# Gate and up projections with the high and low activations side by side in one 512-column matmul, and v in two contraction halves

## The chip, the core and the metric

The kernel runs on one core of a Trainium2 chip. The metric is the device time of one execution in microseconds (us). Engines are named as in the profile: PE is TensorE (matmuls; PEld is its weight load), DVE is VectorE, ACT is ScalarE, POOL is GpSimd, SP is SyncE, which here only issues transfers.

## What is computed

A decoder trunk of two layers on x of 256 tokens by 1024 channels, in float32. Each layer has four token mixers fed by one input projection, sigmoid gates, an output projection, and then a SwiGLU feed-forward part:

```python
for l in range(DEPTH):                       # DEPTH = 2, D = 1024, S = 256, FF_DIM = 2816
    xn = rms_norm(x, norm_mix_g[l])
    proj = xn @ w_in[l]
    xa, q, k, v, zc, xd = jnp.split(proj, splits, axis=-1)      # v: 512 columns
    ...
    merged = (gates[:, :, 0] * (ya @ w_proj_a[l]) + gates[:, :, 1] * (yb @ w_proj_b[l])
              + gates[:, :, 2] * (yc @ w_proj_c[l]) + gates[:, :, 3] * (yd @ w_proj_d[l]))
    x = x + merged @ w_o[l]
    hn = rms_norm(x, norm_ffn_g[l])
    gu = hn @ w_ffn_in[l]                                       # 1024 x 5632
    x = x + (jax.nn.silu(gu[..., :FF_DIM]) * gu[..., FF_DIM:]) @ w_ffn_out[l]
return rms_norm(x, final_norm_g)
```

## The kernel before

Every large product is made of three products in the fp32r type. A weight and an activation are each split into a high part (rounded to fp32r) and a low part (the rest), and the kernel adds hi x hi, hi x lo and lo x hi in PSUM. The weight's high part is a copy by ACT (`split` in the ACT block), its low part a subtraction by DVE (L1077); each is one instruction on 128 x 2048 elements. The activations' parts, `act_hi` and `act_lo`, are made once a layer half (L555, L1100), the feed-forward product's, `ff_hi` and `ff_lo`, once a step (L543 through `ffn_hi`, L1358).

The weights pass through the core in units of 1 MB, 69 a layer, in a ring of three slots (`RING`). For unit u, SP loads `raw` once DVE has split the slot's last tenant (`lo_ready`), ACT makes `w_hi` once PE has used the slot (`w_used`), DVE makes `w_lo`, and PE multiplies. Each engine's order is written out by hand, and each works strictly in that order. A unit whose output is transposed has two halves f of 128 output channels, 8 contraction tiles k of 128 and three matmuls of 256 columns (the tokens) for each, 48 in all (`unit`, L753 to L755 in `mm3`). v and sgu_v come out in token order, with the activations as the stationary operand and 256 weight columns moving (`unit_natural`, L798 to L800); v is units 7 and 8, of 256 columns each.

A layer's order on PE: 11 units of the input projection (banks u % 4), 12 gate units, the branch projections, the last 4 gate units, 4 units of the output projection, then the feed-forward part of 11 steps j. A step is a gate unit, an up unit and a down unit (`ffn_in` twice, `ffn_out`), the down unit one step behind: gate j+1, up j+1, down j. Gate and up use banks 0 and 1 in even steps, 2 and 3 in odd ones; the down units add into banks 4 to 7 through the whole part. Between unit 19 and the last gate units stand the small matmuls of attention, pooling and convolution (`misc`). The pooling and half of the convolution's 31 taps are POOL's (L455, L461, L464, L497 to L510), beginning again with `xa`, which DVE scales out of unit 10's bank; PE transposes the result at unit 20 (L920).

The step-0 gate unit of a layer is multiplied as its activations arrive, in four parts of two contraction tiles (`unit_early`, `unit_pair`). After it comes `norm_stat` (L826, the sum of squares over the channels, from DVE's L1110), after the up unit `norm_rms` (L836, the inverse norm broadcast to all partitions, from DVE's `norm_scale`, L1116 to L1120); ACT copies it to `rms_b`. The norm's factor is applied on the way out of PSUM:

```python
def scaled(out, b, l):
    return V.tensor_tensor(out, low(b), rms_b[:, :, :].to_broadcast([P, 2, S]), ALU.mult)
```

A step's evacuation: DVE scales the gate bank into `ff_g` (L1125), ACT applies Silu in place (L691), DVE scales the up bank into `ff_u`, multiplies (L1353), ACT makes `ff_hi`, DVE `ff_lo`. Between these DVE and ACT split a unit's weights each (`ffn_unit` in both blocks).

## Time and profile before

| | |
|---|---|
| median of 3 runs | 867.55 us (865.9 to 867.69) |
| the profiled execution | 866.84 us, of which 865.2 us span |
| PE busy | 836.9 us, 6971 matmuls |
| DVE, ACT, POOL busy | 610.8, 412.3, 225.5 us |
| granted TensorE clock, mean | 0.991 |
| moved by DMA | 152.3 MB, mean 176 GB/s |

The span is the time from the first to the last recorded instruction. Busy time of PE counts matmuls that overlap once; the duration of one (about 0.28 us) is longer than the distance between the starts of two, since they are pipelined, so the distance of starts is the thing to read. The granted clock is 1.0 at 2.4 GHz and 0.5 at 1.2 GHz. In the views of time, a bracket behind an instruction gives its engine's idle time ahead of it and who ended it; an instruction without one followed at once.

### The profile page before, as it was taken

To read this page: it belongs to the slowest core of one execution; us is meant where nothing else is said; L and a number is where in the kernel's file an instruction comes from. 1 tells how busy PE (TensorE), PEld (TensorE's weight loads), DVE (VectorE), ACT (ScalarE), POOL (GpSimd) and SP (SyncE) were. 2 spreads that over 40 slices of the span, in tenths; PEclk is the share of its full clock that TensorE was granted. 3 is DMA by queue.
4 is the path that set the end of the run, shared out by engine and by line. 5 is a ranking of instruction groups with operands and counts; after the bars stand their busy time and mean duration, and the time that the engine had idled before them with its cause. 6 is when DMAs were issued, how large, how long until landed. Compare 5 with 4: busy or idle time off the path is not lost.

```text
span 865.2 us, 17632 instructions
## 1 busy us (share of the span) xinstructions
PE 836.9 (97%) x6971; PEld 828.1 (96%) x6971; DVE 610.8 (71%) x716; ACT 412.3 (48%) x496; POOL 225.5 (26%) x224
## 2 busy tenths in 40 slices
PE   3999999999999999999989999999999999999995
PEld 3999999999999999999989999999999999999995
DVE  5889988786785556455487999887677665556554
ACT  4554666534554344434365466654346443344332
POOL 7806899156000000000000559952300000000000
PEclk9999999999999999999989999999999999999998
DMA  7694654467465555545447654545645456554621
GB/s 249 197 291 118 185 171 163 147 185 216 145 219 167 177 194 171 207 157 194 148 157 237 189 150 147 147 147 195 195 146 196 160 191 202 176 194 162 208 92 50
DMA packets 124035, 152.30 MB, mean 176 GB/s; under 512 B 3728, under 2 KB 113634, under 8 KB 123968
## 3 DMA queue, kind: packets, MB, share of 16 engines
q1 hardware_dynamic: 121200, 148.38, 53.6%
q0 software_dynamic: 1328, 1.81, 1.0%
q10 hardware_dynamic: 1440, 1.20, 0.5%
q8 instruction: 44, 0.72, 0.3%
q14 instruction: 23, 0.19, 0.1%
HBM read 148.23 MB, written 1.05 MB: 173 GB/s over the span
## 4 chain that ended last, share of the span: by engine, by line
issue 38%; PE 36%; POOL 21%; DMA 2%; POOLq 1%; ACT 1%; DVE 0%; DVEq 0%; ACTq 0%
PE bank L753 12%; PE bank L754 12%; PE bank L755 12%; POOL conv_a L464 7%; POOL gates L461 6%; DMA pool_w<-in_pool_w 2%; POOL gates L503 1%; DMA ifreq<-inv_freq 1%; POOL angles L436 1%; POOL conv_a L455 1%; POOL gates L499 1%; POOL conv_a L510 1%; POOL gates L435 1%; POOL gates L432 0%; POOL rows L476 0%
## 5 line engine op out<-in xcount | busy, mean ns | idle before, releaser
L1077 DVE TENSOR_TENSOR w_lo<-raw,w_hi 128x2048 fp32r<-128x2048 f32 x138 | 328.9, 2385 | 141.9 <-ACT w_hi L543 141.5
L753 PE MATMUL bank<-act_hi,w_hi 128*128 128x256 f32 x1472 | 421.4, 286 | 7.0 <-DVE act_lo L1100 6.6
L754 PE MATMUL bank<-act_lo,w_hi 128*128 128x256 f32 x1472 | 418.2, 284 | 0.0
L755 PE MATMUL bank<-act_hi,w_lo 128*128 128x256 f32 x1472 | 418.0, 284 | 0.0
L543 ACT ACTIVATE w_hi<-raw 128x2048 fp32r<-128x2048 f32 x138 | 263.6, 1910 | 206.9 <-PE bank L755 175.0
L753 PEld LDWEIGHTS bank<-act_hi,w_hi 128*128 128x128 f32 x1472 | 284.1, 193 | 9.3 <-DVE act_lo L1100 7.3
L754 PEld LDWEIGHTS bank<-act_lo,w_hi 128*128 128x128 f32 x1472 | 284.2, 193 | 0.1
L755 PEld LDWEIGHTS bank<-act_hi,w_lo 128*128 128x128 f32 x1472 | 284.1, 193 | 0.0
L754 PE MATMUL bank<-ff_lo,w_hi 128*128 128x256 f32 x352 | 99.1, 282 | 0.0
L753 PE MATMUL bank<-ff_hi,w_hi 128*128 128x256 f32 x352 | 99.1, 281 | 0.0
L755 PE MATMUL bank<-ff_hi,w_lo 128*128 128x256 f32 x352 | 99.0, 281 | 0.0
L753 PE MATMUL bank<-y_hi,w_hi 128*128 128x256 f32 x288 | 81.7, 284 | 0.0
L755 PE MATMUL bank<-y_hi,w_lo 128*128 128x256 f32 x288 | 81.5, 283 | 0.0
L754 PE MATMUL bank<-y_lo,w_hi 128*128 128x256 f32 x288 | 81.5, 283 | 0.0
L455 POOL TENSOR_TENSOR conv_a<-conv_h,par 128x256 f32<-128x256 f32 x2 | 5.4, 2715 | 285.0 <-DVE conv_h L1174 285.0
L464 POOL TENSOR_TENSOR conv_a<-conv_a,gates 128x256 f32<-128x256 f32 x60 | 65.9, 1099 | 4.7
L753 PEld LDWEIGHTS bank<-ff_hi,w_hi 128*128 128x128 f32 x352 | 66.3, 188 | 0.0
L754 PEld LDWEIGHTS bank<-ff_lo,w_hi 128*128 128x128 f32 x352 | 66.3, 188 | 0.0
L755 PEld LDWEIGHTS bank<-ff_hi,w_lo 128*128 128x128 f32 x352 | 66.2, 188 | 0.0
L691 ACT ACTIVATE qk<-qk 128x512 f32<-128x512 f32 x22 | 13.9, 632 | 87.9 <-DVE qk L1125 87.8
L753 PEld LDWEIGHTS bank<-y_hi,w_hi 128*128 128x128 f32 x288 | 55.3, 192 | 0.0
L754 PEld LDWEIGHTS bank<-y_lo,w_hi 128*128 128x128 f32 x288 | 55.3, 192 | 0.0
(191 smaller groups left out, 887.5 us busy)
## 6 DMA issues: line engine op xcount, KB each, us to landing
raw<-in_w_ffn_in SPq DMA_DIRECT2D x44, 1024.0 KB, 5.1
raw<-in_w_gate SPq DMA_DIRECT2D x32, 1024.0 KB, 5.5
raw<-in_w_in SPq DMA_DIRECT2D x22, 1024.0 KB, 7.0
raw<-in_w_ffn_out SPq DMA_DIRECT2D x22, 1024.0 KB, 4.8
raw<-in_w_o SPq DMA_DIRECT2D x8, 1024.0 KB, 5.0
raw<-in_w_proj_b SPq DMA_DIRECT2D x4, 1024.0 KB, 4.9
gates<-qk SPq DMA_DIRECT2D x32, 64.0 KB, 5.6
raw<-in_w_proj_a SPq DMA_DIRECT2D x2, 1024.0 KB, 5.0
```

What stands on the lines that cost most here:

```text
L435: chain(G.tensor_scalar(prod, turns, -c, None, ALU.mult))
L436: chain(G.tensor_tensor(angles[:, :, :], before, prod, ALU.add))
L455: ins = nc.gpsimd.tensor_tensor(conv_a[:, 1, :], src, par[:, c:c + 1].to_broadcast([P, S]), ALU.mult)
L461: nc.gpsimd.tensor_tensor(tmp, src, par[:, c:c + 1].to_broadcast([P, S]), ALU.mult)\
L464: ins = nc.gpsimd.tensor_tensor(conv_a[:, 1, :], conv_a[:, 1, :], tmp, ALU.add)
L499: link(l, nc.gpsimd.tensor_tensor(s8[:, 8:E], s4[:, 1, 8:E], s4[:, 1, 4:E - 4], ALU.add))
L543: return nc.scalar.activation(o, i, ACT.Copy)
L691: nc.scalar.activation(ff_g, ff_g, ACT.Silu).then_inc(silu_done, 1)
L753: nc.tensor.matmul(o, whi, ahi, start=first, stop=False, skip_group_check=skip)
L754: nc.tensor.matmul(o, whi, alo, start=False, stop=False, skip_group_check=skip)
L755: return nc.tensor.matmul(o, wlo, ahi, start=False, stop=last, skip_group_check=skip)
L1077: V.tensor_tensor(w_lo[slot][:, :], raw[slot][:, :], w_hi[slot][:, :].bitcast(F32), ALU.subtract)\
```

## The change

For the gate and up units, `act_hi` and `act_lo` become the two halves of one tile `act2`, next to each other for each k, so that one matmul with the weight's high part moves both, 512 columns, and writes hi x hi into the first half of a bank and hi x lo into the second. The third product, lo x hi, is a matmul of 256 columns added to the first half. Each half f has a bank of its own: gate units always use banks 0 and 1, up units 2 and 3. The two halves of a bank must be added: ACT copies the second halves to SBUF (`ffn_corr`, one copy for each f), DVE adds the first halves to them and multiplies by `rms_b` in an instruction of its own; for up, the factor is applied to the Silu's output instead. `norm_stat` of the feed-forward part moves ahead of the last quarter of the gate unit, `norm_rms` into the middle of the up unit, and their banks become 4 and 7; DVE's `norm_scale` moves ahead of a weight split. v is computed in two units over half of the contraction each, with all 512 weight columns moving, into banks 3 and 0.

```diff
-            ("glu_in", 2304), ("v", 1280), ("v", 1536), ("sgu_u", 1792), ("pool", 0))
+            ("glu_in", 2304), ("v0", 1280), ("v1", 1280), ("sgu_u", 1792), ("pool", 0))
+V_BANK = (3, 0)
-        act_hi = sb("act_hi", [P, KT, S], F32R)
-        act_lo = sb("act_lo", [P, KT, S], F32R)
+        act2 = sb("act2", [P, KT, 2, S], F32R)
+        act_hi, act_lo = act2[:, :, 0, :], act2[:, :, 1, :]
+        def main(b):
+            return banks[:, b:b + 2, 0:S]
+        def corr(b):
+            return banks[:, b:b + 2, S:2 * S]
...
# ACT
+                elif u == 8:
+                    unit_done(l, u)
+                    for t in range(TT):
+                        nc.scalar.activation(v_sb[:, t, :], bank[V_BANK[t]][:, :], ACT.Copy, scale=rms_t[:, t:t + 1])\
+                            .then_inc(bank_free[V_BANK[t]], 1)
+            def ffn_corr(l, slot, use, j, up, first=False):
+                if not first:
+                    act.wait_ge(ffa_ready, l * FF_STEPS + j)
+                o, c = (ff_u, corr(2)) if up else (ff_g, corr(0))
+                act.wait_ge(half_done, l * 2 * FF_STEPS + (2 * j + (2 if up else 1)))
+                copy(o[:, 0, :], c[:, 0, :])
+                act.wait_ge(w_used[slot], l * USES + (use + 2))
+                copy(o[:, 1, :], c[:, 1, :]).then_inc(corr_copied, 1)
+                ffn_corr(l, U_FFN % RING, U_FFN // RING, 0, False, True)
                 split(l, (U_FFN + 3) % RING, (U_FFN + 3) // RING)
                 rms_copy(l, 1)
-                ffn_silu(l, True, -1)
+                ffn_silu(l, 0)
+                ffn_corr(l, (U_FFN + 1) % RING, (U_FFN + 1) // RING, 0, True, True)
                 ffn_hi(l, True, 0)
...
# PE
+            def unit_v(slot, half):
+                hi, lo = (t[:, :].rearrange("p (k n) -> p k n", n=512) for t in (w_hi[slot], w_lo[slot]))
+                for t in range(TT):
+                    ts, o = slice(t * P, t * P + P), bank[V_BANK[t]][:, :]
+                    for k in range(4):
+                        kk = 4 * half + k
+                        nc.tensor.matmul(o, act_hi[:, kk, ts], hi[:, k, :], start=(kk == 0), stop=False)
+                        nc.tensor.matmul(o, act_hi[:, kk, ts], lo[:, k, :], start=False, stop=False)
+                        last = nc.tensor.matmul(o, act_lo[:, kk, ts], hi[:, k, :], start=False, stop=(kk == KT - 1))
+                last.then_inc(w_used[slot], 1)
+            def ffn_half(slot, b, f, ks):
+                hi, lo, fs = kview(w_hi[slot]), kview(w_lo[slot]), slice(f * P, f * P + P)
+                for k in ks:
+                    nc.tensor.matmul(bank[b + f], hi[:, k, fs], act2[:, k, :, :].rearrange("p h s -> p (h s)"),
+                                     start=(k == 0), stop=False, skip_group_check=True)
+                    last = nc.tensor.matmul(main(b)[:, f, :], lo[:, k, fs], act_hi[:, k, :], start=False,
+                                            stop=(k == KT - 1), skip_group_check=True)
+                return last
-                unit(l, slot, b)
+                ffn_half(slot, b, 0, range(KT)).then_inc(half_done, 1)
+                ffn_half(slot, b, 1, range(KT)).then_inc(w_used[slot], 1)
...
-                unit_early(U_FFN % RING, 0, l * 12 + 8)
-                norm_stat(l, 1)
-                ffn_in(l, (U_FFN + 1) % RING, (U_FFN + 1) // RING, 1, 0)
+                for i in range(KT // 2):
+                    pe.wait_ge(act_lo_ready, l * 12 + (8 + i + 1))
+                    if i == 3:
+                        norm_stat(l, 1)
+                    for f in range(2):
+                        last = ffn_half(slot, 0, f, (2 * i, 2 * i + 1))
+                        if f == 0 and i == 3:
+                            last.then_inc(half_done, 1)
+                last.then_inc(w_used[slot], 1)
+                ffn_half(slot, 2, 0, range(KT)).then_inc(half_done, 1)
                 norm_rms(l, 1)
+                ffn_half(slot, 2, 1, range(KT)).then_inc(w_used[slot], 1)
...
# DVE
-                scaled(ff_g, b, l).then_inc(bank_free[b], 1)
+                dve.wait_ge(corr_copied, l * 2 * FF_STEPS + (2 * j + 1))
+                V.tensor_tensor(ff_g, ff_g, main(0), ALU.add).then_inc(bank_free[0], 1)
+                dve.wait_ge(bank_free[0], l * len(BANKS[0]) + (j + (FFN_FROM[0] + 2)))
+                V.tensor_tensor(ff_g, ff_g, rms_b[:, :, :].to_broadcast([P, 2, S]), ALU.mult).then_inc(ffg_ready, 1)
...
+                dve.wait_ge(silu_done, l * FF_STEPS + (j + 1))
+                V.tensor_tensor(ff_g, ff_g, rms_b[:, :, :].to_broadcast([P, 2, S]), ALU.mult).then_inc(ffs_ready, 1)
                 dve.wait_ge(w_used[slot], l * USES + (use + 2))
-                scaled(ff_u, b, l).then_inc(bank_free[b], 1)
+                dve.wait_ge(corr_copied, l * 2 * FF_STEPS + (2 * j + 2))
+                V.tensor_tensor(ff_u, ff_u, main(2), ALU.add).then_inc(bank_free[2], 1)
...
+                    if u == U_FFN - 1:
+                        norm_scale(l, 1)
                     if not U_GATE_D <= u < U_WO - 1:
                         split(l, (u + 3) % RING, (u + 3) // RING)
-                norm_scale(l, 1)
```

## Rows read from the trace of the kernel before

**Rows 1.** The page, busy us of each engine, share of the span, instructions.
```profile
PE 836.9 (97%) x6971; PEld 828.1 (96%) x6971; DVE 610.8 (71%) x716; ACT 412.3 (48%) x496; POOL 225.5 (26%) x224
```

**Rows 2.** PE in order of time, steady state: start us, duration, engine, line, instruction.
```profile
460.22 0.28 PE L753 MATMUL bank<-act_hi,w_hi 128*128 128x256 f32 x1
460.34 0.28 PE L754 MATMUL bank<-act_lo,w_hi 128*128 128x256 f32 x1
```

**Rows 3.** PE at the second layer's start; a stretch's busy times, clock, DMA.
```profile
437.30 0.58 PE L753 MATMUL bank<-act_hi,w_hi 128*128 128x256 f32 x1 [3.42 <-DVE act_lo L1100]
...
437.89 0.41 PE L755 MATMUL bank<-act_hi,w_lo 128*128 128x256 f32 x1
438.11 0.41 PE L753 MATMUL bank<-act_hi,w_hi 128*128 128x256 f32 x1
...
437.30:442.80 5.50, 5.50 (x25) 5.50 (x26) 4.46 (x9) 5.50 (x10) 0.00 (x0) 0.50 0.41 141
```

**Rows 4.** Mixers of layer one: PE, POOL, DVE in time; busy of PE, PEld, DVE.
```profile
87.41 0.68 DVE L1125 TENSOR_TENSOR xa<-bank,rms_b 128x512 f32<-128x512 f32 x1
...
88.17 1.09 POOL L497 TENSOR_TENSOR gates<-xa 128x542 f32<-128x542 f32 x1 [9.17 <-DVE xa L1125]
...
151.81 2.54 POOL L510 TENSOR_TENSOR conv_a<-conv_a,par 128x256 f32<-128x256 f32 x1
...
154.40 0.66 PE L920 MATMUL bank<-ident,conv_a 128*128 128x128 f32 x4 [1.08 <-POOL conv_a L510]
...
62.70:88.10 25.40, 25.40 (x216) 24.92 (x215) 24.40 (x39) 11.86 (x12) 14.39 (x15) 1.00 0.50 150
```

**Rows 5.** Other matmul shapes, in time; a row with x4 runs to its last one's end.
```profile
126.44 0.70 PE L911 MATMUL bank<-gates,pool_w 128*128 128x256 f32 x2
...
126.44 1.13 PE L911 MATMUL bank<-gates,pool_w 128*128 128x256 f32 x4
...
30.69 0.54 PEld L826 LDWEIGHTS bank<-ones,sq 128*128 128x128 f32 x4
```

**Rows 6.** Groups by line and shape: busy us, mean ns | idle before.
```profile
L543 ACT ACTIVATE y_hi<-bank 128x256 fp32r<-128x256 f32 x8 | 3.1, 386 | 0.0
```

**Rows 7.** PE in time: the last matmuls of two successive gate units, a round apart.
```profile
261.53 0.28 PE L755 MATMUL bank<-act_hi,w_lo 128*128 128x256 f32 x1
...
278.74 0.28 PE L755 MATMUL bank<-act_hi,w_lo 128*128 128x256 f32 x1
```

**Rows 8.** DVE and ACT in time in a feed-forward step; a DMA issue's size, landing.
```profile
684.78 0.63 ACT L691 ACTIVATE qk<-qk 128x512 f32<-128x512 f32 x1 [2.96 <-DVE qk L1125]
685.32 1.90 ACT L543 ACTIVATE w_hi<-raw 128x2048 fp32r<-128x2048 f32 x1
687.25 2.29 DVE L1077 TENSOR_TENSOR w_lo<-raw,w_hi 128x2048 fp32r<-128x2048 f32 x1 [2.50 <-ACT w_hi L543]
689.46 0.68 DVE L1125 TENSOR_TENSOR qk<-bank,rms_b 128x512 f32<-128x512 f32 x1
690.31 0.69 DVE L1353 TENSOR_TENSOR qk<-qk 128x512 f32<-128x512 f32 x1 [0.17 <-DVE qk L1125]
...
raw<-in_w_ffn_in SPq DMA_DIRECT2D x15, 1024.0 KB, 5.1
```

**Rows 9.** First gate and up unit of layer one's feed-forward part: PE and DVE.
```profile
243.32 0.28 PE L753 MATMUL bank<-act_hi,w_hi 128*128 128x256 f32 x1
...
249.08 0.50 PE L826 MATMUL bank<-ones,sq 128*128 128x1 f32 x4
...
255.82 0.37 PE L753 MATMUL bank<-act_hi,w_hi 128*128 128x256 f32 x1
...
247.35 0.42 DVE L1110 TENSOR_TENSOR sq<-sq 128x256 f32<-128x256 f32 x1
...
249.90 0.15 DVE L1116 TENSOR_SCALAR st<-bank 128x2 f32<-128x2 f32 x1
...
252.45 0.48 DVE L1120 TENSOR_SCALAR diag<-ident,rms_t 128x128 f32<-128x128 f32 x2
```

More of the change, by code:

```diff
@@ L85 @@
 BANKS = {b: [f"unit{u}" for u in range(U_PROJ_A) if u % 4 == b] + ["A", "B", f"unit{U_GATE_D + b}"] for b in range(4)}
-BANKS[2] += ["stat2"]
-BANKS[3] += ["R2"]
 FFN_FROM = [len(BANKS[b]) for b in range(4)]
-for b in range(4):
-    BANKS[b] += [f"ffn{j}" for j in range(b // 2, FF_STEPS, 2)]
-BANKS[4] = ["S0", "S1", "S2", "S3", "C", "D"]
+for b in (0, 2):
+    BANKS[b] += [f"ffn{j}" for j in range(FF_STEPS)]
+BANKS[4] = ["S0", "S1", "S2", "S3", "C", "D", "stat2"]
 BANKS[5] = ["S0", "S1", "S2", "S3", "cT1", "cT2", "C", "D"]
 BANKS[6] = ["R1", "par", "wsT", "PT0", "PV0", "PT1", "PV1", "PT2", "PV2", "PT3", "PV3", "C", "D"]
-BANKS[7] = ["stat1", "PT0", "F", "PT1", "pool", "PT2", "PT3", "C", "D"]
+BANKS[7] = ["stat1", "PT0", "F", "PT1", "pool", "PT2", "PT3", "C", "D", "R2"]
 ATT = (10, 13, 16, 19)
@@ L215, in build @@
         ssq = sb("ssq", [P, 4])
-        bank = [ctx.enter_context(nc.psum_tensor(f"bank{b}", [P, 512], F32)) for b in range(8)]
+        banks = ctx.enter_context(nc.psum_tensor("bank", [P, 8, 512], F32))
+        bank = [banks[:, b, :] for b in range(8)]
         raw_full = [sem(f"raw_full{s}") for s in range(RING)]
@@ L354, in _ @@
                         swap(l, u - 6)
-                    if u < U_GATE:
+                    if u < U_GATE and W_IN_UNITS[u][0] in ("v0", "v1"):
+                        src = T["w_in"][l].rearrange("(h k p) n -> h p k n", p=P, h=2)
+                        load(l, slot, use, src[u - 7, :, :, 1280:1792], n=512)
+                    elif u < U_GATE:
                         load(l, slot, use, cols(T["w_in"], l, W_IN_UNITS[u][1]))
@@ L564, in rms_copy @@
             def rms_copy(l, n):
-                b, what = (6, "R1") if n == 0 else (3, "R2")
+                b, what = (6, "R1") if n == 0 else (7, "R2")
                 act.wait_ge(rms_done, l * 2 + (n + 1))
@@ L820, in norm_stat @@
             def norm_stat(l, n):
-                b, what = (7, "stat1") if n == 0 else (2, "stat2")
+                b, what = (7, "stat1") if n == 0 else (4, "stat2")
                 bank_wait(l, b, what)
@@ L830, in norm_rms @@
             def norm_rms(l, n):
-                b, what = (6, "R1") if n == 0 else (3, "R2")
+                b, what = (6, "R1") if n == 0 else (7, "R2")
                 bank_wait(l, b, what)
@@ L973, in _ @@
                     weights(l, u % RING, u // RING)
-                    if u < U_PROJ_A or u >= U_GATE_D:
+                    if u == 7:
+                        for t in range(TT):
+                            bank_wait(l, V_BANK[t], f"unit{7 + t}")
+                    elif u != 8 and (u < U_PROJ_A or u >= U_GATE_D):
                         bank_wait(l, u % 4, f"unit{u}")
```

71 lines of the change are left out of this document (37 added, 34 removed).

## The prediction

> **What bounds the kernel now.** The page's busy line comes first: TensorE (PE) is busy for 97% of the span, VectorE (DVE) for 71%, ScalarE (ACT) for 48% [rows 1]. So PE is the bound, unless its matmuls are themselves waiting. The order in time says what they wait for. In the steady state one 256-column matmul starts every 0.12 us, each with a weight load of its own [rows 2], whatever the other engines do: a unit of 48 of them takes 5.76 us. PE stands still only at the ends of stages (3.42 us at the start of the second layer [rows 3], 1.08 us before the convolution's transposes [rows 4]). The time is therefore 0.12 us times the number of matmuls, and the question is what part of the 0.12 is columns.
>
> At half clock (granted 0.50, the 1.2 GHz level) the same matmuls start 0.21 us apart, 437.89 to 438.11 for one [rows 3]: 256 columns at 1.2 GHz are 0.213 us, so there the columns are everything. At 2.4 GHz they would take 0.107 us and the row shows 0.12: 0.013 us is not columns. Two neighbours tell more. The pool projection's 256-column matmuls, on plain fp32 data, are four records where the code has two: the third and fourth add 1.13 - 0.70 = 0.43 us, 0.215 each, a weight load each included [rows 5]. That is twice 0.107 and 0.001 to 0.003 over, so such a record seems to stream at half the column rate, for 0.213 us, and a stream that long hides the next weight load almost wholly. And where only one column streams behind each weight load, three further loads add 0.54 - 0.19 = 0.35 us, 0.117 each [rows 5]. The 0.12 of the 256-column matmul looks like the weight load, which its own 0.107 us of columns does not cover.
>
> **The change part by part.** *Gate and up units, on PE.* Per layer 22 units, each 16 (f, k) pairs; before, three 256-column matmuls a pair, 0.360 us. After, one of 512 columns and one of 256. The trace has no 512-column matmul. Bounds: 0.213 + 0.003 = 0.216 us if the weight load hides as in [rows 5], 2 x 0.12 = 0.240 us if the 0.12 is a rate per column. I take 0.216, the row with an equally long stream. The pair is then 0.216 + 0.120 = 0.336, saving 0.024; 2 x 22 x 16 = 704 pairs give **-16.9 us**. A gate or up unit takes 5.38 us.
>
> The Trainium skill ("TensorE: Matmul & The Clock Gate", Back-to-back issue gap) gives a warm gap of N/2.4 + 2.5 ns. For 512 columns that is 216 ns, as I take from the rows; for 256 it is 109 ns, against which the rows show 120. By that formula alone the pair would go from 327 to 325 ns and the 704 pairs would save 1.4 us. The measured 0.12 decides against it.
>
> *v units, on PE.* 192 matmuls of 256 columns become 96 of 512: 192 x 0.12 - 96 x 0.216 = 2.3 us less, 1.15 a layer (0 at 0.240). They stand ahead of the stall at the convolution's transposes, so what is late there must be asked. PE waits there for GpSimd (POOL), whose chain of taps runs without a gap from 88.17, where it waited for DVE's xa, to 154.35 [rows 4]. That xa (87.41) has no wait in front of it, so its unit was done before, and DVE is busy 24.40 of the 25.40 us from 62.7 on [rows 4]. So xa comes when DVE's queue comes to it, POOL ends when it ended, and PE arrives 1.15 us earlier only to wait 1.15 us longer. **0 us**; if xa did follow PE, -2.3. ACT copies v in two instructions of 512 columns instead of four of 256, two units ahead of the next user of either bank: nothing. The two v loads keep their 1 MB.
>
> *Extra evacuation work in the feed-forward loop.* Before, a step had two scaled copies, product and low part on DVE (4 instructions) beside three weight splits; after, 6. ACT gains four copies of 128x256 from PSUM at 0.386 us (the same shape [rows 6]). By throughput it fits: DVE 3 x 2.29 + 6 x 0.69 = 11.0 us, ACT 3 x 1.90 + 2 x 0.63 + 4 x 0.386 = 8.5 us, against a PE round of 2 x 5.38 + 5.70 = 16.45 us (today's round is 278.74 - 261.53 = 17.21 [rows 7]; less two units of 5.76 that leaves 5.70, rounded, for the down unit). But the two hand over to each other, and that chain I add up from starts in [rows 8]: weight split to the next DVE instruction 2.21; an instruction that the next one depends on 0.86 (689.46 to 690.31 is 0.85); a handover 0.03. Around the round, if both run late: split 2.21, gate add 0.86, times rms 0.69, handover, silu 0.54, ACT split 1.90, handover, DVE split 2.21, times rms 0.61, up add 0.86, product 0.69, handover, high part 0.54, ACT split 1.90, handover, DVE split 2.21, low part 0.61, with five handovers 0.15: **16.0 us**. ACT's copies stand beside DVE's splits and are not in it. 16.0 is under 16.45 with 0.5 to spare, so the loop stays PE's, and lateness shrinks by 0.5 us a round. Cost 0 while that cover lasts; 20 rounds x the excess if not. A slot's next weight load is issued when DVE has split the last and lands 5.1 us later [rows 8]; ACT wants it 16.45 - 2.21 - 1.90 = 12.3 us later: nothing.
>
> *First gate and up unit of a layer.* Two waits are new, and PE stands behind both.
> (a) norm_stat now sits ahead of the last quarter of the gate unit. The unit starts at 243.32; three quarters take 12 x 0.336 = 4.03, until 247.35. The sum of squares ends on DVE at 247.35 + 0.42 = 247.77 [rows 9]. PE waits about 0.5 us; before, the statistics came at 249.08 and waited for nothing [rows 9].
> (b) Gate and up had four banks in turn, now the gate has only 0 and 1, so step 1's gate waits until step 0's is added up. DVE: norm_scale needs 252.93 - 249.90 = 3.0 us [rows 9] from about 248.45 (no longer behind a split), to 251.5; two splits of 2.21 to 255.9; add 0.69 to 256.6. PE: statistics from 247.8 (0.36), quarter 1.34, up unit 5.38, norm_rms and zeros 0.54: ready at 255.5. It waits 1.1 us; step 1's gate starts at 256.7 instead of 255.82 [rows 9]. norm_rms in mid-unit (PE there at 252.3) does not wait for the diagonal (251.5).
> After that, lateness is about 2.3 us, and the tightest deadline is the split for the second loop step's up unit, due 0.3 us after it is ready: no stall. Together 1.6 us a layer, **+3.2 us**. Against 0 if DVE were earlier by that much, and 2 x 1 more if a split came in between.
>
> The sum: -16.9 + 0 + 3.2 = -13.7 us. The profiled execution took 866.84 us (865.2 span and 1.6 around it), 0.7 below the median of the runs, 867.55, inside their spread of 1.8. I carry the difference to the median: 867.55 - 13.7 = **853.9 us**.
>
> **The rivals.**
> *Weight switch adds.* Each matmul pays 0.013 us beyond its columns, however long: 0.227 + 0.120 = 0.347 a pair, 9.4 us saved, new waits 1.2 a layer by the steps of (a) and (b), since PE comes to them later: 867.55 - 9.4 + 2.4 = 860.5. Against it: the 0.215 of [rows 5] and the half-clock 0.213, where nothing is added; but those streams read a column more slowly than 2.4 GHz.
> *A rate per column.* Reading 4-byte columns while a weight load reads too caps the stream at 256 in 0.12 us: 0.240, nothing saved on PE, waits of 0.85 a layer by (a) and (b): 867.55 + 1.7 = 869.2. Against it that 0.12 and the bare loads' 0.117 are so close; for it that 0.12 is more than 0.117. The Trainium skill (same page, Part 2, first step) says that PE has two independent read ports and that a weight load steals nothing from the stream, which speaks against this rival; no row here tests it.
> *The DVE-ACT chain bounds the loop (the side of slower).* Place: the ten rounds of each layer. The time is 867.55 + 1.7 + 20 x (R - 17.21), R the chain's round, 17.21 today's round on PE, 1.7 the step-0 units with their waits. From R = 16.45 up it takes from the gain; from 17.13 the kernel is slower. If the two pairs of copies (4 x 0.36) fell into the chain, R = 17.4: 873. For it: the margin is 0.5 in 16; against it: 1.1 us more would be needed, and every term has its row.
> *The clock.* After the 3.42 us wait the granted clock was 0.50 for 5.5 us [rows 3], about 26 matmuls at 0.21 instead of 0.12, 2.4 us. The same wait comes at another moment now; if the clock stays up, 851.5; if it falls once more at the new waits, 856 or so.
> *v counts* (xa follows PE): 851.6.
>
> **How the numbers follow.** Forecast 0.50; clock stays up 0.10; v counts 0.08; switch adds 0.12; rate per column 0.09; chain bound 0.11, about half of that with R under 17.1. Measurement tells some 0.2% (1.7 us) from no change. Faster: 0.50 + 0.10 + 0.08 + 0.12 + 0.06 = 0.86. Of the column rate's 0.09, 0.04 is same and 0.05 slower; with the rest of the chain's 0.05, slower is 0.10. The range runs from 850.5 (clock or v) to 861.5 (switch adds) and leaves out the column rate and most of the chain case.
>
> **What would show it.** Right: 512-column matmuls in the gate units with 0.216 us to the next start and 0.12 after the 256-column one; a feed-forward round of 16.4 to 16.5 us on PE, without PE waits; PE waits of 0.5 us for the sum of squares and about 1.1 us for DVE at step 1; xa and the last POOL tap where they were, and 2.3 us rather than 1.1 us of wait before the transposes. Wrong: 0.227 or 0.240 as the step; PE waiting on w_lo in every round; xa earlier by 1.1 us.

## The result, and the profile after

The changed kernel takes 861.98 us (median of four runs, 861.15 to 862.99), the kernel before on the same chip 867.12 (865.9 to 867.69). The ratio is 0.9943, with a 95% interval of 0.9926 to 0.996. So it is faster by 5.1 us, where 13.7 were forecast, and the time lies just above the range. The profiled execution took 862.99 us, 861.4 of it the span; that of before had a span of 865.2, so the traces differ by 3.8 us. One execution of the kernel before in a later session took 1011.96 us at a mean granted clock of 0.756; it enters no ratio given here.

The page's busy line, the one of [rows 1]:

```profile
PE 829.7 (96%) x6171; PEld 786.5 (91%) x6171; DVE 636.7 (74%) x760; ACT 442.1 (51%) x580; POOL 226.0 (26%) x224
```

There are 800 matmuls fewer (704 in the gate and up units, 96 in v), and TensorE is busy for only 7.2 us less. PE in order of time in the loop, against [rows 2] (start us, duration, engine, line, instruction), and the last matmuls of two successive gate units, against [rows 7]:

```profile
418.16 0.39 PE L847 MATMUL bank<-act,w_hi 128*128 128x512 f32 x1
418.39 0.28 PE L849 MATMUL bank<-act,w_lo 128*128 128x256 f32 x1
418.50 0.39 PE L847 MATMUL bank<-act,w_hi 128*128 128x512 f32 x1
...
297.71 0.28 PE L849 MATMUL bank<-act,w_lo 128*128 128x256 f32 x1
...
314.51 0.28 PE L849 MATMUL bank<-act,w_lo 128*128 128x256 f32 x1
```

From the 512-column matmul to the next start it is 0.23 us (median of all 0.230), from the 256-column one 0.117: a pair takes 0.347 us. It took 0.360 and was forecast at 0.336. A round takes 16.80 us, where it was 17.21 [rows 7]. The list of PE's waits (what waited, for whom: us in total, times, the longest) has the turn and the kernel's start, the convolution and step 0 of either layer, and nothing that recurs in the rounds of the loop. Two waits are not shown: 9.5 us for the first transfer at the kernel's start (9.9 before), and one of 0.3 us for w_lo:

```profile
PE bank L781 <- DVE act L1167: 7.8, 3, 4.4
PE bank L970 <- POOL conv_a L523: 3.9, 2, 2.2
PE bank L847 <- DVE qk L1407: 0.9, 2, 0.5
```

Counted by starts of matmuls, the two traces part as follows. The rows add up to 3.6 us; the first matmul of layer 1 comes 0.4 us earlier too (16.19 for 16.56 us), and 0.2 us are lost in small amounts elsewhere, which gives the 3.8 us between the spans.

| Stretch on PE | before, layers 1, 2 | after, layers 1, 2 | difference |
|---|---|---|---|
| first gate matmul of the loop to the layer's last matmul | 177.78, 177.79 | 173.87, 173.62 | -8.1 |
| the two v units | 11.95, 11.95 | 11.37, 11.37 | -1.1 |
| wait before the convolution's transposes | 1.36, 1.39 | 2.49, 1.93 | +1.7 |
| from these transposes to the last output-projection matmul | 88.80, 88.80 | 90.27, 88.79 | +1.5 |
| from there to the loop's first gate matmul (step 0) | 12.62, 12.61 | 13.39, 13.38 | +1.5 |
| wait at the turn from layer 1 to 2 | 3.70 | 4.64 | +0.9 |

**Mixers**, against [rows 4]: DVE's xa, the last POOL tap, PE's transposes behind it, and a stretch (busy us of PE, PEld, DVE, ACT, POOL, then clock, DMA share, GB/s).

```profile
87.70 0.69 DVE L1192 TENSOR_TENSOR xa<-bank,rms_b 128x512 f32<-128x512 f32 x1
...
152.08 2.54 POOL L523 TENSOR_TENSOR conv_a<-conv_a,par 128x256 f32<-128x256 f32 x1
...
154.67 0.66 PE L970 MATMUL bank<-ident,conv_a 128*128 128x128 f32 x4 [2.21 <-POOL conv_a L523]
...
156.00:159.40 3.40, 3.40 (x19) 3.40 (x18) 2.84 (x18) 1.08 (x3) 0.00 (x0) 0.50 0.74 292
```

xa and POOL's end stand where they stood, 0.3 us later. PE comes earlier and waits longer. In layer 1 the clock is then granted at half from 156.0 to 159.4, which the trace of before has not; that is the 1.47 us in the fourth line of the table.

**Step 0**, against [rows 9]: PE at its two new waits, and DVE (the sum of squares; two weight splits, x2; the add that frees bank 0).

```profile
249.19 0.28 PE L849 MATMUL bank<-act,w_lo 128*128 128x256 f32 x1
249.58 0.61 PE L876 MATMUL bank<-ones,sq 128*128 128x1 f32 x4
...
257.65 0.25 PE L1085 MATMUL bank<-zeros 128*128 128x1 bf16 x4
258.33 0.50 PE L847 MATMUL bank<-act,w_hi 128*128 128x512 f32 x1 [0.43 <-DVE qk L1407]
...
249.10 0.42 DVE L1177 TENSOR_TENSOR sq<-sq 128x256 f32<-128x256 f32 x1
...
253.19 4.49 DVE L1144 TENSOR_TENSOR w_lo<-raw,w_hi 128x2048 fp32r<-128x2048 f32 x2
257.60 0.68 DVE L1407 TENSOR_TENSOR qk<-qk,bank 128x512 f32<-128x512 f32 x1
```

Wait (a) is 0.39 - 0.12 = 0.27 us, wait (b) 0.43.

**The turn of the layer**, against [rows 3]: first the kernel before (PE's last matmul of layer 1, ACT, DVE), rows that do not stand above.

```profile
433.60 0.28 PE L755 MATMUL bank<-ff_hi,w_lo 128*128 128x256 f32 x1
...
424.07 0.63 ACT L543 ACTIVATE ff_hi<-qk 128x512 fp32r<-128x512 f32 x1 [4.07 <-DVE qk L1353]
429.04 1.28 ACT L543 ACT_TABLE_LOAD   x1 [4.34 <-issue]
430.33 1.92 ACT L543 ACTIVATE w_hi<-raw 128x2048 fp32r<-128x2048 f32 x1
...
432.28 2.29 DVE L1077 TENSOR_TENSOR w_lo<-raw,w_hi 128x2048 fp32r<-128x2048 f32 x1 [6.86 <-ACT w_hi L543]
434.49 0.68 DVE L1084 TENSOR_TENSOR x_res<-bank,x_res 128x512 f32<-128x512 f32 x1
```

And the changed one, with PE's first matmul of layer 2 and the stretch of [rows 3]:

```profile
432.20 0.28 PE L783 MATMUL bank<-ff_hi,w_lo 128*128 128x256 f32 x1
436.84 0.58 PE L781 MATMUL bank<-act,w_hi 128*128 128x256 f32 x1 [4.36 <-DVE act L1167]
...
424.27 0.63 ACT L556 ACTIVATE ff_hi<-qk 128x512 fp32r<-128x512 f32 x1 [2.76 <-DVE qk L1422]
428.58 1.28 ACT L556 ACT_TABLE_LOAD   x1 [3.67 <-issue]
429.87 1.92 ACT L556 ACTIVATE w_hi<-raw 128x2048 fp32r<-128x2048 f32 x1
...
431.82 2.29 DVE L1144 TENSOR_TENSOR w_lo<-raw,w_hi 128x2048 fp32r<-128x2048 f32 x1 [6.19 <-ACT w_hi L556]
...
436.90:442.60 5.70, 5.70 (x27) 5.70 (x28) 4.67 (x9) 5.70 (x10) 0.00 (x0) 0.50 0.39 138
```

PE ends layer 1 at 432.20, 1.40 us before its time in the kernel before, but starts layer 2 only 0.46 us earlier. The chain that it waits for does not start at PE's end: ACT's last high part (424.27, as late as before), a gap named "issue", a table load, the next layer's first w_hi, DVE's w_lo, and only then DVE's updates of x.

### The profile page after: what moved, and what is told of

Same layout as the page of the kernel before. It is cut to its first block, busy times and chain, and to the rows that moved or that the text cites. A ratio compares the mean times of both kernels' runs of the same rounds, so it can differ in the third digit from the quotient of the medians.

```text
span 861.4 us, 16276 instructions
## 1 busy us (share of the span) xinstructions
PE 829.7 (96%) x6171; PEld 786.5 (91%) x6171; DVE 636.7 (74%) x760; ACT 442.1 (51%) x580; POOL 226.0 (26%) x224
## 4 chain that ended last, share of the span: by engine, by line
issue 40%; PE 32%; POOL 22%; DMA 2%; DVE 2%; POOLq 1%; ACT 1%; DVEq 0%; ACTq 0%
PE bank L847 8%; POOL conv_a L477 7%; PE bank L782 6%; PE bank L783 6%; PE bank L781 6%; POOL gates L474 6%; PE bank L849 4%; DMA pool_w<-in_pool_w 1%; POOL gates L516 1%; POOL gates L532 1%; POOL angles L449 1%; DMA ifreq<-inv_freq 1%; POOL conv_a L468 1%; POOL gates L512 1%; POOL conv_a L523 1%
## 5 line engine op out<-in xcount | busy, mean ns | idle before, releaser
L847 PE MATMUL bank<-act,w_hi 128*128 128x512 f32 x704 | 246.4, 393 | 0.9 <-DVE qk L1407 0.9
L781 PE MATMUL bank<-act,w_hi 128*128 128x256 f32 x768 | 222.7, 290 | 8.1 <-DVE act L1167 7.8
L782 PE MATMUL bank<-act,w_hi 128*128 128x256 f32 x768 | 219.8, 286 | 0.0
L783 PE MATMUL bank<-act,w_lo 128*128 128x256 f32 x768 | 219.5, 286 | 0.0
L849 PE MATMUL bank<-act,w_lo 128*128 128x256 f32 x704 | 197.2, 280 | 0.0
L781 PEld LDWEIGHTS bank<-act,w_hi 128*128 128x128 f32 x768 | 149.8, 195 | 10.5 <-DVE act L1167 8.4
L847 PEld LDWEIGHTS bank<-act,w_hi 128*128 128x128 f32 x704 | 131.8, 187 | 29.5 <-DVE qk L1407 1.1
L782 PEld LDWEIGHTS bank<-act,w_hi 128*128 128x128 f32 x768 | 149.9, 195 | 0.1
L783 PEld LDWEIGHTS bank<-act,w_lo 128*128 128x128 f32 x768 | 149.9, 195 | 0.0
L849 PEld LDWEIGHTS bank<-act,w_lo 128*128 128x128 f32 x704 | 133.0, 189 | 0.0
L556 ACT ACTIVATE qk<-bank 128x256 f32<-128x256 f32 (+1 forms) x96 | 37.1, 393 | 74.1 <-PE bank L849 74.0
```

Of the source, the lines that this page charges most:

```text
L556: return nc.scalar.activation(o, i, ACT.Copy)
L781: nc.tensor.matmul(o, whi, ahi, start=first, stop=False, skip_group_check=skip)
L782: nc.tensor.matmul(o, whi, alo, start=False, stop=False, skip_group_check=skip)
L783: return nc.tensor.matmul(o, wlo, ahi, start=False, stop=last, skip_group_check=skip)
L847: nc.tensor.matmul(bank[b + f], hi[:, k, fs], act2[:, k, :, :].rearrange("p h s -> p (h s)"), start=(k == 0), stop=False, skip_group_check ...
L849: last = nc.tensor.matmul(main(b)[:, f, :], lo[:, k, fs], act_hi[:, k, :], start=False, stop=(k == KT - 1), skip_group_check=True)
```

## The experiments

Theory: a 512-column matmul costs 0.227 to 0.230 us, so the change is worth about 8 us on PE, and three places give some of it back: the convolution's wait with its clock, step 0, and the turn (the way from the end of layer 1 to the first matmul of layer 2). The rivals are named in the expectations. Each kernel was timed beside the kernel before, whose median was 867.2 to 868.0 in these sessions; where two edited kernels are from different sessions, their ratios are the better comparison.

### The change in halves

ffn_only is the changed kernel with the v units as before, v_only the kernel before with the v change alone.

```
- ("glu_in", 2304), ("v", 1280), ("v", 1536), ...
+ ("glu_in", 2304), ("v0", 1280), ("v1", 1280), ...   (v_only; ffn_only the reverse)
```

> The changed kernel with v computed as before (two units of 256 columns, banks 3 and 0 one after the other). Theory A (v's gain is taken back at the wait for POOL before the convolution's transposes, and the longer wait there lets TensorE's clock fall in some executions): as fast as the changed kernel or up to 1.5 us faster, 860.5 to 862; the wait ahead of the transposes 1.1 to 1.8 us again instead of 1.9 to 2.5; the granted clock stays 1.0 there. Rival B (v's 1.3 us count): 863.3.

Measured: 862.34 us, ratio 0.9945 (0.9923 to 0.9967).

> The kernel before with the v units alone changed. Theory A: no gain, 867 to 868.5, the wait ahead of the convolution's transposes longer by 0.65 us a layer, which is what v saves on TensorE (96 matmuls at 0.227 instead of 192 at 0.120 us). Rival B: 865.8, the wait unchanged.

Measured: 867.98 us, ratio 1.0002 (0.9989 to 1.0015). PE at the transposes of v_only, and the same kind of stretch as above:

```profile
154.69 0.69 PE L938 MATMUL bank<-ident,conv_a 128*128 128x128 f32 x2 [2.23 <-POOL conv_a L514]
...
154.50:157.70 3.20, 3.01 (x14) 3.01 (x15) 1.79 (x10) 2.29 (x6) 0.14 (x1) 0.50 0.60 209
```

The whole gain is that of the gate and up units. The time of ffn_only lies between its two theories (up to 862, and 863.3), so it is the traces that decide for A. The v units' 0.58 us a layer go into the wait: it is 2.51 and 1.89 us in v_only, as in the changed kernel, and 1.38 and 1.34 in ffn_only, as before. Where the wait is long, the half clock follows it in layer 1; in ffn_only it does not come.

### The width alone

narrow is the changed kernel with its 512-column matmul cut in two again; bank layout, copies and order stay.

```
- matmul(bank[b + f], hi[:, k, fs], act2[:, k, :, :])
+ matmul(bank[b + f][:, 0:S], hi[:, k, fs], act_hi[:, k, :])
+ matmul(bank[b + f][:, S:2 * S], hi[:, k, fs], act_lo[:, k, :])
```

> The changed kernel in which the 512-column matmul of the gate and up units is two of 256 columns again, into the same two halves of the same banks, with all of the new evacuation and waits kept. Theory A (the whole gain is one weight switch less in each of 704 pairs, 0.013 us each, and the rest of the change costs some 2 to 4 us): about 871, 9 us over the changed kernel and 3 to 4 over the kernel before; TensorE's feed-forward round 17.2 us again. Rival B (part of the gain comes from elsewhere, such as fewer PSUM writes shared with the readers): nearer to 867.

Measured: 869.21 us, ratio 1.0018 (1.0003 to 1.0033). The width is worth 869.21 - 861.98 = 7.2 us by the medians, 6.5 by the ratios, and everything else in the change together costs 1.8 (before took 867.38 in that session). That is less than the 9 that theory A expected and more than rival B allows. The trace is clearer: from the loop's first gate matmul to the layer's last matmul narrow takes 177.81 and 177.80 us, as the kernel before, where the changed kernel takes 173.87 and 173.62, so the loop's 8.1 us are the width's and nothing else's. Its step 0 takes 13.38 us as in the changed kernel, its turn 4.71 where that has 4.64, and the clock falls behind the convolution's wait as well: none of the three hangs on the width.

### What a matmul costs by its width

sweep is the changed kernel with 24 more matmuls of each width ahead of the last transposes (these add some 40 us).

```
+ for i in range(24):
+     matmul(bank[0][:, 0:N], w_hi[0] (k = i % 8, 128 columns), act2[:, i % 8, 0:N], start=True, stop=True)
```

> The changed kernel with 264 more matmuls in front of the last transposes, whose results nobody uses: 24 each of 64, 128, 192, 256, 320, 384, 448 and 512 columns with 128-column weights, then 256 and 512 columns with 64-column weights, and 256 with 32. It measures the distance of starts against width. Theory A (each switch of weights adds 0.013 us to the stream): N/2.4 ns + 13 wherever that is over the weight load's own 0.11 us: 0.147 us at 320, 0.173 at 384, 0.200 at 448, 0.227 at 512, and 0.110 to 0.117 at 64 to 192. Rival C (the 0.12 at 256 columns is the weight load's length, and 512 is slow for another reason, such as a whole bank): 0.136 at 320, 0.163 at 384, 0.189 at 448, then a step to 0.227. With weights of 64 columns: 0.120 again if the handover costs, 0.109 if the load's length does. Time about 40 us above the changed kernel.

The groups in order of time; a group's start less that of the group before, by 24, is the distance of two starts.

```profile
854.83 2.87 PE L1110 MATMUL bank<-act,w_hi 128*128 128x192 f32 x24
857.54 3.05 PE L1112 MATMUL bank<-act,w_hi 128*128 128x256 f32 x24
860.42 3.69 PE L1114 MATMUL bank<-act,w_hi 128*128 128x320 f32 x24
863.95 4.32 PE L1116 MATMUL bank<-act,w_hi 128*128 128x384 f32 x24
868.11 5.12 PE L1118 MATMUL bank<-act,w_hi 128*128 128x448 f32 x24
873.07 5.65 PE L1120 MATMUL bank<-act,w_hi 128*128 128x512 f32 x24
878.55 2.89 PE L1122 MATMUL bank<-act,w_hi 128*64 128x256 f32 x24
```

192 columns: 0.113 us; 256: 0.120; 320: 0.147; 384: 0.173; 448: 0.207; 512: 0.228. From 256 to 384 and at 512 the distance is the columns at 2.4 GHz and 0.013 us more (448 stands 0.007 above that, unexplained). Below 256 it stays at 0.111 to 0.113 (64 and 128 columns gave the same): that is the floor which the bare loads of [rows 5] show. So the 0.120 of a 256-column matmul is 0.107 and 0.013, and a longer matmul keeps the 0.013: a weight load that 256 columns fail to cover would be covered by 320, and rival C's 0.136 there is not met. The load is not without effect, though. With 64 weight columns instead of 128 its record lasts 134 ns instead of 188 to 192, and the distance at 256 columns falls to 0.113 (the sweep's theories had 0.120 or 0.109), while at 512 it stays at 0.229.

sweep2 asks what the 0.013 us are: the same groups with one condition changed at a time.

```
  L1107 512 columns, as above          L1109 512, the same weights each time
  L1111 256, the same weights          L1113 512, 64 rows of contraction
  L1115 512, round four banks          L1117 256, round four banks
  L1119 512, bf16 data                 L1121 256, bf16 data
```

> The changed kernel with eight groups of 24 more matmuls ahead of the last transposes, to measure the distance of their starts: 512 columns as in the first sweep; 512 and 256 columns with the same weights each time; 512 with 64 rows of contraction; 512 and 256 going round four banks; 512 and 256 on bf16 data. Theory A (0.013 us beyond N/2.4 is charged to each matmul, whatever stands around it): 0.227 in all the 512 groups and 0.120 in the 256 ones, with the same weights too. Rival B (it is the switch of weights): 0.214 and 0.107 with the same weights. Rival C (it is the output bank being started anew): 0.214 and 0.107 where the banks go round. Rival D (it belongs to the 4-byte type): bf16 at 0.214 to 0.216 and 0.107 to 0.109.

The changes of one condition, and the weight loads of the second group:

```profile
850.80 5.64 PE L1107 MATMUL bank<-act,w_hi 128*128 128x512 f32 x24
856.27 5.60 PE L1109 MATMUL bank<-act,w_hi 128*128 128x512 f32 x24
861.72 3.03 PE L1111 MATMUL bank<-act,w_hi 128*128 128x256 f32 x24
864.68 5.73 PE L1113 MATMUL bank<-act,w_hi 64*128 64x512 f32 x24
...
879.01 5.13 PE L1119 MATMUL bank<-act,w_hi 128*128 128x512 bf16 x23
883.97 2.78 PE L1121 MATMUL bank<-act,w_hi 128*128 128x256 bf16 x24
886.59 1.91 PE L1129 MATMUL bank<-ident,x_res 128*128 128x128 f32 x16
...
856.05 5.40 PEld L1109 LDWEIGHTS bank<-act,w_hi 128*128 128x128 f32 x24
```

With the same weights each time it stays at 0.227 (5.45 / 24); 64 rows and four banks have the same median, 0.227, and 256 columns stay at 0.120 in both forms. Only bf16 is shorter: 4.96 / 23 = 0.216 and 2.62 / 24 = 0.109. So rival D has the numbers: the 0.013 goes with the 4-byte data, and neither new weights, the bank nor the rows matter. Two things stay open. "The same weights" still means a load in front of every matmul (24 in the last row), so no run here has fp32r matmuls without a load between them. And the bf16 groups change the weights' type with the moving data's: their loads last 97 ns instead of 188. Whether the 0.013 hangs on the moving data or on the load of 4-byte weights is therefore not shown; at 512 columns the load's length alone doesn't make it, by the 0.229 with 64 weight columns. The prediction's rival "weight switch adds" had the right number, under a name that these runs neither confirm nor exclude. The Trainium skill ("TensorE: Matmul & The Clock Gate", Back-to-back issue gap) gives N/2.4 + 2.5 ns for a single isolated matmul; the bf16 rows agree to the nanosecond (216 and 109), the kernel's fp32r matmuls don't (227 and 120).

### The convolution's wait

In later and later_before the transposes and the LayerNorm behind them stand one unit further on, in the changed kernel and in the one before.

```
- if u == 20:   (PE: transposes cT1; DVE: LayerNorm of the convolution)
+ if u == 21:
```

> The changed kernel with one step moved: the two transposes of the convolution (PE waits there for GpSimd), and the LayerNorm of the convolution on VectorE, stand behind unit 21 instead of unit 20. Theory A (the wait for GpSimd before these transposes, 2.49 and 1.93 us after the change, is what takes back what the v units give, and the half clock from 156.0 us, worth 1.47 us, hangs on it): the waits go to under 0.2 us, the clock stays up between 150 and 160 us, and the time falls by 2.49 + 1.93 + 1.47 = 5.9 us, from 862.0 to about 856. Rival B (the chain through VectorE's LayerNorm, about 5.9 us against one unit of 5.76 us, takes the wait's place one or two units on): a wait of 0.5 to 2 us for VectorE before the second pair of transposes, and 858 to 861. Rival C (the half clock comes for another reason): it stays near 150 to 160 us, and the time is about 857.5.

Measured: 857.52 us (857.34 to 857.62), ratio 0.9886 (0.9862 to 0.9911).

> The kernel before with the same step moved by one unit. Theory A: the waits of 1.36 and 1.39 us go, and no clock was lost there before, so 2.75 us: from 867.1 to about 864.4; the gap between the two kernels with the step moved is then 8.4 us instead of 5.1. Rival (a new wait for VectorE one unit on): 865.5 to 867.

Measured: 862.9 us, ratio 0.9947 (0.9933 to 0.996).

The list of PE's waits in later has no entry for POOL any more, and a stretch over the place has the full clock:

```profile
PE bank L781 <- DVE act L1167: 7.8, 3, 4.8
...
157.00:161.00 4.00, 4.00 (x37) 4.00 (x36) 2.04 (x6) 2.34 (x3) 0.00 (x0) 1.00 0.99 334
```

Theory A holds in mechanism: waits and half clock are gone, and no new wait for DVE takes their place. Between the changed kernel and later the medians differ by 4.5 us, of the 5.9 expected. In the traces the stretches from the v units to the output projection become shorter by 5.8 us; against that, the wait at the turn is 5.10 us here instead of 4.64. later_before gained more than its waits (4.6 us by its ratio and between the traces, against 2.75). In the trace 2.6 us are those waits; the other 2.0 are at the turn, whose wait is 0.5 us shorter and is followed by 3.4 us of half clock instead of 6.8 (1.0 us), and at the kernel's start, where no half clock falls. How these 2.0 hang together with the moved step is open. The two kernels with the step moved are 5.4 us apart instead of the 8.4 expected, because the turn's wait is 1.86 us longer in later (5.10 against 3.24), and, in the traces (4.9 us apart), because the clock at the kernel's start is at half for 6.8 us in that of later, which costs 0.7 us, and not in that of later_before.

### Is v worth something then?

both_no_v is the kernel both of the next section with the v units as before the change, the same edit as in ffn_only; both_again is both once more, on the same chip.

> The changed kernel with both edits (transposes one unit later, updates of x ahead of the split at the turn) but with the v units as before the change. Theory A (the v change was worth nothing only because TensorE then waited longer for GpSimd; with that wait gone it is worth what the units save, 0.68 us in each layer): about 1.4 us slower than the same kernel with v changed, so 857.1 against 855.7. Rival B (the v change is worth nothing wherever the wait is): 855.7.

> The kernel with both edits once more, as the pair of the two others on the same chip: 855.7 if nothing differs from the run before.

Measured: 857.32 us without the v change (855.62 to 858.44), 856.47 with it (855.43 to 856.54). PE's stretch from the first matmul of layer 2 to the loop's first gate matmul is 237.32 us without and 236.75 with it: 0.57 us, which is what the v units save in a layer (11.95 to 11.37 us). The medians have the same sign, but their runs overlap, so that v is worth something once the wait is gone rests on the trace rather than on the times.

### The turn of the layer

marks is the changed kernel with a tiny ScalarE copy at the bottom and one at the top of the layer loop's body.

```
  with act.Fori(0, L) as l:
+     activation(mark[:, 0:1], ones[:, 0:1], ACT.Copy)
      split(l, 0, 0)
      ...
+     activation(mark[:, 1:2], ones[:, 0:1], ACT.Copy)
```

> The changed kernel with one tiny ScalarE copy as the last instruction of the layer loop's body and one as its first, ahead of the wait for the next layer's first weights. Theory A (ScalarE's gap of 3.67 us at the turn is the way back over the loop's body): the copy at the bottom stands right behind the last ff_hi, the copy at the top 3.5 to 4.5 us later with the table load before it, and the first split of weights right behind that. Rival B (ScalarE waits for the weights' transfer, which the profile doesn't name): the top copy stands within 0.5 us of the bottom one, and the gap lies behind it.

ACT in order of time:

```profile
422.30 0.63 ACT L557 ACTIVATE ff_hi<-qk 128x512 fp32r<-128x512 f32 x1 [2.76 <-DVE qk L1426]
422.84 0.19 ACT L767 ACTIVATE mark<-ones 128x1 f32<-128x1 f32 x1
426.66 1.28 ACT L723 ACT_TABLE_LOAD   x1 [3.63 <-issue]
427.95 0.21 ACT L723 ACTIVATE mark<-ones 128x1 f32<-128x1 f32 x1
428.06 1.90 ACT L557 ACTIVATE w_hi<-raw 128x2048 fp32r<-128x2048 f32 x1
```

The gap lies between the bottom and the top, and the weights' split follows at once, so it is no wait for the weights. ACT spends 3.63 us at the turn itself (on what, the profile doesn't say) and 1.28 on a table, after its last high part. The kernel took 860.81 us in its one run, no longer than the changed kernel.

If x_update no longer stands behind the split, the chain to PE is shorter. both has the moved transposes and three updates ahead of the split; xone has one.

```
- split(l, 0, 0); then for i in range(4): x_update(l, 0, i) ...
+ for i in range(3): y_wait(l, i); x_update(l, 0, i)      (xone: i = 0 alone)
+ split(l, 0, 0); xg_lo(l, 0, 0); then the rest
```

> The changed kernel with the transposes one unit later and, at the turn of a layer, VectorE's first three updates of x (which wait only for TensorE) ahead of its split of the next layer's first weights (which waits for ScalarE's gap and table load). Theory A (at the turn TensorE waits for a chain that starts at VectorE's split, fixed by ScalarE's gap after the last ff_hi and not by TensorE's end): x_update no longer waits for the split, the turn's wait falls from 4.64 to about 2.8 us (split's end + 0.9 us), and the time is about 856 - 1.8 = 854. Rival B (the updates and norm inputs are a chain of their own, as long as the wait): the wait stays above 4 us, time as with the first edit alone, about 856. Rival C (the half clock that follows the wait gets shorter with it): another 1 to 3 us less.

Measured: 855.69 us (854.95 to 857.49), ratio 0.9862 (0.9837 to 0.9887).

> The kernel before with both edits. Theory A (turn and convolution gave back part of the change's gain): the turn's wait goes from 3.70 to about 2.8 us less than a microsecond above or below that of the changed kernel with the same edits; time about 867.1 - 2.75 - 1.5 = 862.9, and the change is worth about 8.5 us between the two edited kernels, near what its loop saves (3.91 + 4.17 us) plus the v units (1.36) less step 0 (1.53). Rival B (the gain is lost for another reason): the gap stays at 5.1 us.

Measured: 862.94 us, ratio 0.9948 (0.9928 to 0.9968).

> The changed kernel with the transposes one unit later and only the first update of x ahead of VectorE's split of a layer's first weights, the first low part straight behind it. Theory A (TensorE's first matmul of a layer hangs on the split's end + 0.9 us; at the kernel's start the split waits for nothing but that one update): first matmul at 15.5 to 16 us (16.1 in the kernel with one edit, 19.0 with three updates ahead), the turn's wait 2.9 to 3.2 us instead of 5.1, time about 857.5 - 2 to 2.5 = 855.2. Rival B (the later updates, now behind the split, starve TensorE's second pair): waits of 0.5 to 1 us within the first unit, 856 to 857.

Measured: 856.88 us, ratio 0.9878 (0.9858 to 0.9898).

> The kernel before with the same two edits. Theory A: the turn's wait goes from 3.2 to 2.6 us and the start gains 0.3 us: 862.9 - 0.9 = 862.0; between the two edited kernels then 6.8 us. Rival B (the turn gives back nothing of the change's gain): 862.9 - 2.2 = 860.7 and 5.4 us between them, as with one edit.

Measured: 862.33 us, ratio 0.994 (0.9922 to 0.9958).

PE's first matmul of layer 2, first in later, then in both:

```profile
433.90 0.58 PE L781 MATMUL bank<-act,w_hi 128*128 128x256 f32 x1 [4.82 <-DVE act L1167]
```

```profile
434.02 0.39 PE L781 MATMUL bank<-act,w_hi 128*128 128x256 f32 x1 [2.84 <-DVE act L1167]
```

From start to start the wait falls from 5.10 to 3.12 us in both, to 3.03 in xone, and from 3.24 to 2.63 in both_before and 2.00 in xone_before: theory A on the turn is right, in mechanism. But the kernel's own start goes through the same lines, and there the three updates wait for the input's transposes: the first matmul comes at 19.0 us in both, 16.1 in later, 15.7 in xone. That is 2.9 us in both's trace, more than the 2.0 saved at the turn, and the expectation had not counted it. In xone the start is saved, but the later updates are late for PE's next pairs (rival B; in the trace 0.40 and 0.70 us between starts instead of 0.12 at the turn, 0.63 and 0.94 at the kernel's start, and 1.2 us twice at the turn of xone_before). So the order brings 0.6 us (xone) to 1.8 us (both) against later, at the edge of what the runs can tell. Between the edited kernels the change is worth 7.25 us (both) and 5.45 us (xone), each difference uncertain by some 2 us. Expected were 8.5 and 6.8; rival B of the xone pair, that the turn gives back nothing of the gain, had 5.4. In the traces the pairs are 4.3 and 5.4 us apart, with the turn's wait still 0.5 and 1.0 us longer in the changed kernels. So it is shown that the wait at the turn follows from VectorE's order behind ScalarE's gap and not from where PE ends; that these edits set the change's gain free is not shown.

### Step 0 as it was

all3 is both with the FFN's first step in the old form, its matmuls 256 columns wide, into banks 0 and 2.

```
- ffn_half(...) for gate and up of step 0, with ffn_corr on ACT
+ unit_early(slot, 0, l * 12 + 8); norm_stat(l, 1); unit(l, slot, 2); norm_rms(l, 1)
```

> The changed kernel with both edits and step 0 of the FFN as it was before the change: 256-column matmuls into one bank each, no separate correction copies, the norm's sum behind the gate unit. Theory A (in step 0 the new form costs more than it saves: 13.39 us instead of 12.62 from the last output-projection matmul to the first gate matmul of the loop): 0.77 us less in each layer, 1.5 us in all, about 854.2, with that stretch at 12.6 us. Rival B (the loop's first correction copies now come late and give a wait of their own): 855 to 857.

Measured: 857.81 us (856.3 to 859.44), ratio 0.9887 (0.9865 to 0.9909), so not under the 856.47 of both on the same chip. PE at the loop's first gate matmul:

```profile
256.90 0.50 PE L848 MATMUL bank<-act,w_hi 128*128 128x512 f32 x1 [1.12 <-DVE qk L1185]
```

Theory A falls: the stretch is 13.88 us, not 12.6, since the one gate bank pair must be emptied after step 0 in the old form too, and DVE gets to it later. The price of step 0 is that of the single bank pair behind DVE's two splits, not that of the wide matmuls: narrow has none of these and takes the same 13.38 us as the changed kernel.

## Why the prediction was wrong

**Term (i), the 512-column matmul, is the step that failed.** Taken at 0.216 from the row with an equally long stream [rows 5]; it measured 0.227 to 0.230, the pair 0.347. The 704 pairs then save 704 x 0.013 = 9.2 us, not 16.9, and the loop's part of it is measured at 8.1. The reading of [rows 5] was at fault in two ways. The plain fp32 records there stream 256 columns in 0.215, which says nothing of the fp32r type of the gate and up units. And the 0.12 was laid to the weight load because it was near the bare loads' 0.117; the sweep puts that floor at 0.111, and the 0.120 is columns and 0.013, an amount that wider matmuls keep. The rival "weight switch adds", given 0.12, had the pair right (0.347) and the time 1.5 us too low; that the switch is what adds is not shown. This term alone is 7.7 us of the miss. Beside the sum, the pair by the formula that the prediction quotes goes from 327.5 to 325.0 ns, so it gives 1.8 us over 704 pairs, not 1.4; no part of the forecast rests on that.

**v at 0.** Right as a sum of the wait and the units, and v_only shows it (1.0002). The size was off (0.58 a layer, not 1.15, by the same term), and one consequence stood only among the rivals: the longer wait was followed by a half clock in layer 1, +1.5 us. In layer 1 the wait grew by 1.13 us, more than v saved, since POOL ended 0.3 us later and PE had begun the layer 0.4 us earlier.

**The loop's cover** held: PE has no wait in it, the round is 16.80 us, and DVE and ACT with a chain added up to 16.0 keep up. But the two end the layer no earlier than before, and what hangs on their end, the next layer's first weights, does not move with PE. The prediction followed the chain inside the loop and not across the turn: +0.9 us.

**Step 0** was forecast at 1.6 us of waits a layer, beside a saving counted in (i). Measured, (a) is 0.27 us, forecast at 0.5, and (b) 0.43, forecast at 1.1: the wide matmuls take longer than forecast, so PE comes to both later. The stretch as a whole grew by 0.77, the two units' saving of 32 x 0.013 = 0.42 us included, so 1.2 us a layer, as the rival's sum had it. The 0.5 beside the two waits is in part that each first 512-column matmul after a small one has 0.31 to 0.34 us to the next start instead of 0.23, three times a layer (0.3). But PE does not set this stretch: narrow, where neither that nor the 0.42 exists, takes the same 13.38 us with a wait (b) of 0.3.

In all: 13.7 forecast, less 7.7 for (i), less 1.5 for the convolution's clock, less 0.9 for the turn, less 0.5 because v's wait grew by more than v saved, plus 0.8 for smaller waits of step 0, is 3.9 us, near the 3.8 of the traces and under the 5.1 of the medians. The range ended at 861.5 because it joined the switch rival only with its own waits and never with a new half clock or the turn.

The best kernel of the study is both, at 855.69 and 856.47 us in two sessions (0.9862 and 0.9861 of the kernel before). The turn's 0.94 us can be read from the rows above: PE ends layer 1 earlier by 1.40 us, ACT's last high part comes 0.20 later, and ACT's gap is 0.67 shorter (3.67 for 4.34), which leaves 0.93. Why the gap is shorter is open.

The medians deserve some care. The same program, the kernel before, took 865.0 to 870.8 us in 58 executions over these sessions, a spread as wide as the gain of 5.1. Its executions with a mean granted clock of 0.994 or more took 865.9 us (median), those with 0.991 or less 868.3. So part of the spread is how much half clock an execution happens to get, and a difference of a microsecond or two between single traces can be that.

## What to carry to other kernels

When two matmuls are joined into one, only the part of the distance between starts that isn't columns can be saved, and one width does not tell that part: take the slope from two widths of the same data type, not from a neighbour of another type. What is saved on the bound engine arrives only where the chains at the ends of stages start from that engine; follow each wait at a stage's end back to what starts it before counting the gain. An engine that comes earlier to a fixed wait can lose its clock on top. To learn what an extra costs, take it alone into the kernel with the old width, as narrow did: it showed at once that step 0 and the turn did not hang on the width.

## What the runs showed of the hardware that was not expected

- A matmul on fp32r data behind a weight load of its own takes its columns at 2.4 GHz and 0.013 us, from 256 columns up (0.120, 0.147, 0.173, 0.227; 448 columns 0.207), whether or not weights or bank change, and with 64 contraction rows as with 128; on bf16 data and bf16 weights it is 0.002 to 0.003 (0.216, 0.109). Below 256 columns the distance stays at 0.111 to 0.113.
- With 64 or 32 weight columns instead of 128 the starts of 256-column matmuls are 0.113 us apart (median of the sweep's group of 24) instead of 0.120; at 512 columns nothing is gained (0.229).
- ScalarE takes 3.6 to 4.3 us from the last instruction of its long layer loop to the first of the next turn, and a table load of 1.28 us with it.
- After waits of PE of 2.49 to 5.17 us in the middle of the kernel the clock was mostly granted at 0.50, for 3.4 or 6.8 us; after 2.63 us (both_before), 2.94 (all3) and one of 2.51 (sweep) it was not. Waits of 2.23 us and less were never followed by it. A wait of 4.7 to 5.2 us was followed by 6.8 us of half clock in some kernels (sweep, marks, sweep2) and by 3.4 in others (narrow, later); what decides is open.
- Half clock at the turn has this price: the stretch from the first matmul of layer 2 to the v units takes 41.38 us where none falls (both_before), 42.87 with 3.4 us of it (both_again) and 43.89 with 6.8 (before).
